# Row terms of the delta rule made inside the projection stage, and norm sums kept in PSUM

## What is computed

```python
def second_block(x, p, ...):
    h = _layer_norm(x, ln_in_g, ln_in_b)
    proj = h @ w_in
    pool_in, qkv, z, beta_raw, a_raw, gate_a, gate_b = jnp.split(proj, SPLIT_POINTS, axis=-1)
    y_a = _multiscale_pool(pool_in, pool_w, pool_scale)
    y_b = _gated_deltanet(qkv, z, beta_raw, a_raw, conv_w, a_log, dt_bias, o_norm_w)
    mixed = sigmoid(gate_a) * y_a + sigmoid(gate_b) * y_b
    h = _layer_norm(DEEPNORM_ALPHA * h + mixed @ w_out, ln1_g, ln1_b)
    mlp = square(relu(h @ w_up)) @ w_down
    r = DEEPNORM_ALPHA * h + mlp
    return _layer_norm(r + sigmoid(r @ ple_gate_w) * (p @ ple_proj_w), ln2_g, ln2_b)
# in _gated_deltanet: qkv = silu(causal depthwise conv of 4 taps(qkv)); q, k = l2norm of each head
# in _chunk_gated_delta_rule, per head and chunk of tokens:
    decay = jnp.exp(jnp.where(incl, gc[..., :, None] - gc[..., None, :], -jnp.inf))
    m = jnp.where(strict, einsum(kb, k) * decay, 0.0)
    sol = triangular_solve(m + eye, rhs)
    attn = jnp.einsum('bnhid,bnhjd->bnhij', q, k) * decay
```

## Time and profile before

| | us |
|---|---|
| median of 3 runs | 2988.53 (2985.65 to 2990.17) |
| the profiled execution's own time | 2987.68 |
| its span, first to last instruction | 2985.9 |
| PE busy | 2782.0 (93%) |
| DVE busy | 1712.9 (57%) |
| POOL busy | 1079.2 (36%) |
| ACT busy | 1017.5 (34%) |
| mean granted share of the TensorE clock | 0.967 |

### The profile page before, as it was taken

One profiled execution on the slowest core, in us unless ns is written; L12 is line 12 of the kernel. 1 busy time (PEld: TensorE's weight loads), 2 busy tenths in 40 slices (PEclk: granted clock), 3 DMA queues, 4 the chain that ended last, 5 costly groups with the idle time before them and its releaser, 6 DMA issues.

```text
span 2985.9 us, 38787 instructions
## 1 busy us (share of the span) xinstructions
PE 2782.0 (93%) x13322; PEld 2288.4 (77%) x13322; DVE 1712.9 (57%) x2608; ACT 1017.5 (34%) x1754; POOL 1079.2 (36%) x467
## 2 busy tenths in 40 slices
PE   7998899899999988979998999999899999999997
PEld 5877788877878866868887777877577778778775
DVE  6968876675424267546665854435723447653364
ACT  3223555553222234443324421111424553211133
POOL 3433100043444443434342444444332114444443
PEclk9997799999999999989999999999899999999999
DMA  3232100023323222221112222222131112222222
GB/s 125 93 110 71 36 15 22 8 92 114 99 91 99 91 97 66 80 78 68 50 47 70 92 88 90 98 91 89 61 109 57 50 50 92 92 91 92 93 97 85
DMA packets 66297, 234.33 MB, mean 78 GB/s; under 512 B 7515, under 2 KB 9860, under 8 KB 66188
## 3 DMA queue, kind: packets, MB, share of 16 engines
q1 hardware_dynamic: 58752, 213.94, 21.7%
q10 hardware_dynamic: 7436, 18.95, 1.9%
HBM read 228.61 MB, written 2.16 MB: 77 GB/s over the span
## 4 chain that ended last, share of the span: by engine, by line
issue 68%; POOL 16%; PE 14%; DVE 1%; POOLq 1%; ACT 0%; DMA 0%; DVEq 0%; ACTq 0%
POOL w_lo L402 16%; PE bank L2249 3%; PE bank L2251 3%; PE bank L2250 3%; PE bank L2725 2%; PE bank L2714 2%; POOLq L406 0%; PE bank L2642 0%; PE bank L2763 0%; PE bank L2701 0%; PE bank L2749 0%; PE bank L2764 0%; PE bank L2698 0%; PE bank L2820 0%; POOLq L401 0%
## 5 line engine op out<-in xcount | busy, mean ns | idle before, releaser
L402 POOL TENSOR_TENSOR w_lo<-raw,w_hi 128x1024 fp32r<-128x1024 f32 x406 | 1006.8, 2480 | 1871.5 <-ACT w_hi L486 1732.0
L2249 PE MATMUL bank<-act,w_hi 128*128 128x512 f32 (+1 forms) x3192 | 1290.4, 404 | 102.4 <-POOL w_lo L402 26.1
L2251 PE MATMUL bank<-act,w_lo 128*128 128x512 f32 (+1 forms) x3192 | 1258.8, 394 | 0.0
L2250 PE MATMUL bank<-act,w_hi 128*128 128x512 f32 (+1 forms) x3192 | 1258.6, 394 | 0.0
L2249 PEld LDWEIGHTS bank<-act,w_hi 128*128 128x128 f32 x3192 | 616.8, 193 | 264.0 <-issue 94.5
L486 ACT CAST w_hi<-raw 128x1024 fp32r<-128x1024 f32 x405 | 424.6, 1048 | 934.6 <-PE bank L2251 933.5
L2251 PEld LDWEIGHTS bank<-act,w_lo 128*128 128x128 f32 x3192 | 616.8, 193 | 128.6
L2250 PEld LDWEIGHTS bank<-act,w_hi 128*128 128x128 f32 x3192 | 617.8, 194 | 118.4 <-issue 2.9
L1448 DVE TENSOR_TENSOR X<-X,bank 128x512 f32 x56 | 38.5, 687 | 250.3 <-PE bank L2251 250.1
L1790 DVE CAST act<-tmp 128x512 f32 x64 | 142.8, 2230 | 10.0 <-DVE tmp L1786 5.2
L1560 DVE SCALAR_TENSOR_TENSOR bank<-big,cols,bank 128x512 f32<-128x512 f32 x174 | 115.3, 746 | 0.0
(11 more groups left out here) (382 smaller groups left out, 2892.0 us busy)
## 6 DMA issues: line engine op xcount, KB each, us to landing
raw<-in_w_dram SPq DMA_DIRECT2D x406, 512.0 KB, 3.3
act_f<-head_rows ACTq DMA_DIRECT2D x8, 768.0 KB, 4.2
out_dram<-X ACTq DMA_DIRECT2D x4, 512.0 KB, 2.7
cst<-in_consts_dram ACTq DMA_DIRECT2D x3, 648.5 KB, 3.9
X<-in_x_dram ACTq DMA_DIRECT2D x2, 512.0 KB, 6.4
X<-in_x_dram SPq DMA_DIRECT2D x2, 512.0 KB, 6.2
X<-big ACTq DMA_DIRECT2D x8, 128.0 KB, 2.3
X<-in_x_dram ACTq DMA_DIRECT2D x4, 256.0 KB, 3.6
```

The lines of the kernel that those rows point to most:

```text
L402: pool.tensor_tensor(w_lo[:, u], raw[:, u].rearrange("p (k n) -> p k n", k=KT), w_hi[:, u].bitcast(F32), ALU.subtract).then_inc(w_lo_ready, 1)
L2249: pe.matmul(o, l_hi, r_hi, start=start, stop=False)
L2250: pe.matmul(o, l_hi, r_lo, start=False, stop=False)
L2251: return pe.matmul(o, l_lo, r_hi, start=False, stop=stop)
```

## The change

Three things are changed.

1. In the projection of q, k and v the convolution accumulates in PSUM banks 6 and 7 instead of `tmp`. `LAG` goes from 5 to 3, the sums of squares follow units 4 to 19 instead of 6 to 21, and the logarithm moves from k = 22 to k = 19. The last two chunks are convolved singly, each after its own copy (`conv4_alone`). The 12 transposes move from after unit 23 to after unit 21 (bank 4 takes the place of bank 6). ACT instead of DVE copies the three rows, and it writes them out at k = 21. Both `load_rows` move into k = 22, behind the copy of unit 22 and the split of the next stage's first unit. Three exponentials of small tiles (`decays`) move behind the last silu, and the sign change of `BE` behind head 0.
2. Head h waits for `silu_done` of 17 + h, its own value chunk, instead of for all 24. The waits for the pool weights move from ahead of head 0's transposes to the first pool unit.
3. The running sums of the norms are in banks 5 and 7; only the last addition writes `stat`. The pivot is read from bank 6 with a factor of -1/128 in the same instruction, so `pivot_row` goes away. The factor of the shifted norms and of the first norm is written to bank 7.

```diff
-                rstd()
+                rstd(dst=bank[7][:])
...
-                LAG = 5
+                LAG = 3
...
+                    if k == 22:
+                        split_hi(U + 2, U % 2)
+                        a.wait_ge(rows_out, 16)
+                        load_rows(0)
+                        load_rows(1)
                     if k >= LAG:
                         silu(k - LAG)
-                    if k == 22:
+                    if k == 19:
                         tables(LOG_EXP)
                         a.wait_ge(l2_sum, 16)
                         a.activation(HT[:, 5:7].rearrange("p x q h -> p (x q h)"), bank[5][:, 0:64], ACT.Ln,
                                      bias=const(2, "eps")).then_inc(lr_done, 1)
-                        a.wait_ge(rows_made, 2)
-                        a.activation(BE, BE, ACT.Exp)
-                        a.activation(EGLAST, GL, ACT.Exp)
-                        a.activation(EGLC, EGLC, ACT.Exp).then_inc(decays, 1)
                         tables(SILU)
+                    if k == 21:
+                        a.wait_ge(rows_tr, 1)
+                        for x in range(3):
+                            a.copy(ROWS[0:8, x], bank[2 + x][0:8, :]).then_inc(rows_kept, 1)
+                        a.wait_ge(rows_kept, 3)
+                        a.dma_start(head_rows, ROWS[0:8]).then_inc(rows_out, 16)
...
-                a.wait_ge(silu_done, 24)
-                load_rows(0)
-                load_rows(1)
                 row_decay(0)
                 decay(0)
+                a.wait_ge(decays, 1)
...
-                    v.tensor_tensor(stat[:, 1], stat[:, 1], tmp[:, k % 2], ALU.add).then_inc(sq_added, 1)
+                    v.tensor_tensor(stat[:, 1] if k == KT - 1 else bank[7][:], bank[7][:], tmp[:, k % 2], ALU.add).then_inc(sq_added, 1)
...
-                    v.tensor_tensor(stat[:, 0], stat[:, 0], src[:, k], ALU.add).then_inc(x_summed, 1)
+                    v.tensor_tensor(stat[:, 0] if k == KT - 1 else bank[5][:], bank[5][:], src[:, k], ALU.add).then_inc(x_summed, 1)
...
-                v.tensor_tensor(X[:, k], X[:, k], row, ALU.subtract).then_inc(shifted, 1)
+                v.scalar_tensor_tensor(X[:, k], bank[6][:], -1.0 / P, X[:, k], ALU.mult, ALU.add).then_inc(shifted, 1)
...
-                        v.tensor_tensor(X[:, k], X[:, k], stat[:, 1], ALU.mult).then_inc(x_scaled, 1)
+                        v.tensor_tensor(X[:, k], X[:, k], bank[7][:], ALU.mult).then_inc(x_scaled, 1)
...
-                    v.scalar_tensor_tensor(SHIFTED_1[:, k], X[:, k], col(1, "g_final", k), row, ALU.mult,
+                    v.scalar_tensor_tensor(SHIFTED_1[:, k], X[:, k], col(1, "g_final", k), bank[6][:], ALU.mult,
...
-                    if 6 <= k < 22:
-                        length_squares(k - 6)
+                    if 4 <= k < 20:
+                        length_squares(k - 4)
...
+                    if k == 21:
+                        pe.wait_ge(rows_made, 2)
+                        for q in range(TT):
+                            pe.transpose(bank[2][0:8, q * P:q * P + P], S1[:, q], ident)
+                            pe.transpose(bank[3][0:8, q * P:q * P + P], S2[:, q], ident)
+                            ins = pe.transpose(bank[4][0:8, q * P:q * P + P], GC[:, q], ident)
+                        ins.then_inc(rows_tr, 1)
...
-                        pe.wait_ge(silu_done, 24)
+                    pe.wait_ge(silu_done, 17 + h)
```

113 lines of the change are left out of this document (57 added, 56 removed).

## The result

| | before | after |
|---|---|---|
| median of 4 runs each, on the same chip | 2989.35 us (2985.65 to 2991.14) | 2962.22 us (2958.76 to 2964.87) |
| ratio | | 0.991, 95% interval 0.9893 to 0.9927 |
| profiled execution, time and span | 2987.68, 2985.9 us | 2964.87, 2963.1 us |

The changed kernel is faster by 27.1 us by the medians and by 22.8 us by the two profiled executions. The direction came out as forecast, and each part gained by the mechanism that was named for it.

The account below looks back on a forecast made before the run. The bound was taken to be head 0's row chain (rows in DRAM, load, POOL, ACT), plus PE's waits around norms. Row terms 13.5 and norms 4.7 us sum to 18.2: 2987.7 - 18.2 = 2969.5 us, range 2964 to 2977.

Parts of the forecast that it names:

- Part 1: Row terms at the end of block 2's projection: `decay` of head 0 starts earlier, gain 13.5 us, between 10.8 and 14.1.
- The two stalls: PE waits for low parts at units 21 and 23 of the projection, costing 1.35 and 0.5 us, inside the 13.5.
- POOL's 8.3 us: POOL's six row operations ahead of head 0's `decay` were taken to last 8.3 us, as in the old trace.
- the step on the rows: Row load issued at 1310.5, 4.5 us to POOL, 8.3 on it: `decay` at 1323.4 instead of 1337.48, 14.1 us earlier.
- the 0.6 us for sharing the DMA engines: Row load now meets weight loads on the same DMA engines: price between nothing and 3.3 us, taken as 0.6.
- The step on silus: At LAG 3 silus find their convolution done; the per-head wait on silus brings nothing of its own.
- The convolution in PSUM: Projection taps get short and the first tap longer, both within DVE's idle time: worth nil to the sum.
- Part 2: Norms with one input in PSUM: additions and multiplications lose their stretch, gain 4.7 us, between 2 and 8.
- the end of block 1: Gained chunk unstretched fits in a unit, so DVE's backlog ahead of the mean goes: 3.0 us.
- the 0.9 us: Norm after w_out_2: one multiplication falls from 2.85 us to 0.68; of 2.2 us 0.9 is taken, between 0 and 2.
- The extension that I gave to the range downwards: Rival: head 0's levels run at a higher clock, their 22 us shrink by 1 to 3, 2966 to 2968; chance 0.10.
- The other rivals: Row load or stalls cost more, 2974 to 2978 (0.17); PSUM lifts no stretch, 2975 (0.05); ACT holds up projection, 2993 (0.04).

Follow-up runs that it names:

- The last kernel: Changed kernel with three orders altered: splits of units 21 and 23 earlier, a POOL row step later, head 0's decay ahead of three exponentials; 2962.8 us, ratio 0.9917.
- another run: Changed kernel with the load of the first two heads' rows issued behind the last silus again; 2973.9 us, ratio 0.9957.
- both halves of this one: Last down projection of block 1: kernel before with only the shift row in PSUM, 2986.65 us; changed kernel with only that row back in SBUF, 2969.5 us.

## Why the prediction was right or wrong

**Part 1, 13.5 us predicted, 15.1 measured.** The two stalls, the moved squares and POOL's 8.3 us came as computed. I set the clocks equal at the start of the projection, where that of before is 2.7 us ahead; then `decay` starts at 1322.5; the sum had 1324.0. Two terms of the step on the rows were off. The issue of the load was put behind copy and split, at 1310.5; it left at 1309.7, although the copy came 0.6 us later than computed, since ACT's queue hands a DMA on while the arithmetic ahead of it still runs. That is 0.8 us. And the 0.6 us for sharing the DMA engines was not paid by these rows: POOL started 4.35 us after the issue, against 4.5 for a load that ran alone. The weight load behind it paid, with 6.3 us from issue to landing in place of a median of 3.3, and nothing waited for it here. The last kernel suggests that this was luck of some tenths of a us: with the weight load first the rows took 0.9 longer. The upper end of 14.1 assumed an unshared load but not an earlier issue. The step on silus was right: the wait per head brings nothing, and the last silu, waiting for DVE's taps until 1316.96, ends with its table load and exponentials just ahead of POOL. One sign in the list of what would show it was miscounted: `decay` "some 15 us after the issue", where the sum itself has 13.5; it came 12.8 us after.

**The convolution in PSUM, worth "nil" to the sum.** Right only as the sum was built: with accumulators in SBUF the six POOL operations meet the last taps and take 10.3 us. I had named this dependence for the low part of 2.39 us but not for the 8.3, which I read from a stretch of before in which DVE was idle.

**Part 2, 4.7 us predicted, 8 to 9.5 measured.** The step that failed is the first one, the end of block 1, 3.0 us against 6.4. The wait for the mean fell from 5.4 to 2.4 as computed, and that was the whole of the term. The rest is 2.8 us of waits on the low part, from 3.0 to 0.2, and some 0.6 us that no wait accounts for. The fault is in the very first section: "nothing in the change speeds the split of a weight unit where it ends last". I took the 26.1 us of waits on the low part as a block; 3.0 of them, in five pieces under 1 us, lay in this stage, and were the same backlog of DVE, passed on by ACT. The prediction knew that the chunk was at 2168 ns; it lacked the addition 2.17 + 0.69 + 0.68 + 0.69 + 0.68 = 4.9 us a chunk, and the length of this stage's unit, 4.1 us.

The smaller terms: the wait behind w_out_2 that the 0.9 us stood for did fall, by 1.2 us, from 3.0 to 1.8; how much of it reached the time can't be told, since the length of that stretch varies by more. The 0.8 us ahead of block 1's convolution norm did go, and was given back 20 us later, where PE waited 2.46 us for a low part in place of 1.42: the stretch 627 to 1082 is as long as before. For the embedding and the norm behind it I had nothing; it is 0.7 us in the embedding and 0.8 in the first units of block 3, and 1.5 more by the clock in most traces. For block 1's start I had left half a microsecond to the range, and no run settles it.

**The rivals.** The extension that I gave to the range downwards rested on head 0 running faster at a higher clock. It did not decide: the wait ahead of the first level and the stalls account for the 15.1 us, and the other heads take 266 us in all kernels. The other rivals are refuted: the load landed sooner, not later; PSUM lifts the stretch; ACT never starved the projection, neither with taps at 750 ns nor, in the run with SBUF accumulators, at up to 2926.

With the terms as measured the sum would have been 2987.7 - 15.1 - 8 to 9.5, 2963 to 2964.6. That is still above the median of 2962.2; the difference is within the variation of the runs.

## What to carry to other kernels

Before a group of waits is dismissed, split it by stage, and for every stage compare each engine's work per tile with PE's unit there: an engine that runs without a pause at 4.9 us against 4.1 sets the pace of all, even where PE's waits are under 1 us and carry another engine's name. Where two engines keep each other out of SBUF, an edit of some of the instructions that can meet the other engine only moves the collision to those that are left, as both halves of this one did. A wait that ends last hides others: the 11.5 us on the silus were worth nothing, the issue of one DMA 10 us.

## What the runs showed of the hardware that was not expected

- A DMA issue in ACT's program leaves when its semaphores allow, ahead of arithmetic that stands before it in the program: at 1307.01 with the copy running since 1306.92 and the split not begun, and 0.6 us ahead of a table load in another run. With the issue ahead of the split in the program, the split started 0.46 us later relative to the copy.
- The stretch falls on POOL too: six row operations took 8.3 us beside an idle DVE (before) and beside taps with their accumulator in PSUM (after), and 10.3 beside taps with two SBUF inputs; a low part 2.69 in place of 2.40.
- The first tap, one SBUF input and a scalar, went from 484 ns to a median of 753 with its result in PSUM. The Trainium skill's "VectorE: DVE Perf Modes", section "Why PSUM operands drop a tier", has it that an fp32 instruction with a PSUM operand runs at single rate, which agrees in direction. It costs 24 x 0.27 us of DVE, all of it behind idle time.
- PE's granted clock falls for pieces of a few matmuls at places that change from trace to trace in the same code, worth some 1.6 us each; in the stretch 260 to 627 us traces of the same code differ by up to 4.7 us.
